# The first expert pair's tokens by a matrix product, three weight loads with other waits, and the combine between a pair's gates

## What is computed

```python
def hier_moe(h, rg_w, rg_b, re_w, re_b, w_gate, w_up, w_down):   # h = rmsnorm(x, ln_ffn)
    lg = tf @ rg_w + rg_b;  grp = argmax(lg)                      # one group of 4
    top_v, top_i = lax.top_k(le, 2)                               # two of its 8 experts
    combine = sum(one_hot(eid, 32) * (g1 * g2)[..., None])        # weight of each expert for each token
    for e in range(N_EXPERTS):                                    # 32 experts, D_MODEL 1024, D_EXPERT 512
        hid = silu(t @ w_gate[e]) * (t @ w_up[e])
        acc = acc + combine[:, e:e + 1] * (hid @ w_down[e])
    return acc
```

## Time and profile before

| | us |
|---|---|
| median of 3 runs (lowest, highest) | 820.41 (819.87, 823.77) |
| the profiled execution, its time | 821.48 |
| the profiled execution, its span | 819.8 |
| PE busy | 772.7 (94%) |
| DVE busy | 270.4 (33%) |
| ACT busy | 158.6 (19%) |
| POOL busy | 139.1 (17%) |
| queue q1 (SP's), share of the 16 DMA engines | 74.1% |

### The profile page before, as it was taken

The page is one execution under the profiler, slowest core; times in us unless marked ns, Lnnn a source line. Parts: engine busy times, 40 slices in busy tenths (PEclk is TensorE's granted clock), DMA queues, the critical chain, the costliest instruction groups (busy, mean ns, idle before and its releaser), DMA issues.

```text
span 819.8 us, 8712 instructions
## 1 busy us (share of the span) xinstructions
PE 772.7 (94%) x3488; PEld 372.7 (45%) x3488; DVE 270.4 (33%) x614; ACT 158.6 (19%) x313; POOL 139.1 (17%) x167
## 2 busy tenths in 40 slices
PE   4999999989999999889999999999998999899996
PEld 3777677758743334544333333333333333333332
DVE  2059999995355632521111101110110111011001
ACT  3211121234541101300211111111111111101114
POOL 2069899702002000010000000000000000000000
PEclk9999999999999999989999999999999999999999
DMA  9894200041508189989999999999999999999981
GB/s 275 301 350 166 103 20 0 2 110 41 167 26 265 57 276 348 419 320 427 426 426 426 427 429 424 427 429 425 426 426 428 426 426 427 427 428 426 429 335 65
DMA packets 51256, 249.58 MB, mean 304 GB/s; under 512 B 6966, under 2 KB 24406, under 8 KB 38655
## 3 DMA queue, kind: packets, MB, share of 16 engines
q1 hardware_dynamic: 45540, 243.54, 74.1%
q10 hardware_dynamic: 3147, 2.67, 1.1%
q0 software_dynamic: 2528, 2.79, 1.1%
HBM read 246.87 MB, written 8.61 MB: 312 GB/s over the span
## 4 chain that ended last, share of the span: by engine, by line
PE 71%; DVE 4%; issue 3%; ACT 2%; DMA 0%; DVEq 0%; ACTq 0%; POOLq 0%
PE bank L1177 27%; PE bank L1200 14%; PE bank L1051 9%; PE bank L1218 8%; PE bank L1160 2%; PE bank L1189 1%; PE bank L1024 1%; PE bank L1015 1%; DVE bank L1571 1%; PE bank L788 1%; PE bank L1178 1%; PE bank L1040 1%; PE bank L885 1%; DVE bank L1600 1%; DVE region_a L1570 1%
## 5 line engine op out<-in xcount | busy, mean ns | idle before, releaser
L788 PE MATMUL bank<-region_a,ring 128*128 128x320 f32 x576 | 158.7, 437 | 0.5 <-DVE region_a L1570 0.5
L1178 PE MATMUL bank<-ring,zz 128*64 128x512 f32 x304 | 135.3, 601 | 0.0
L788 PEld LDWEIGHTS bank<-region_a,ring 128*128 128x128 f32 x576 | 109.8, 192 | 46.5 <-issue 2.2
L1177 PE MATMUL bank<-ring,zz 128*64 128x512 f32 x272 | 122.9, 608 | 8.6 <-issue 8.0
L1570 DVE TENSOR_TENSOR region_a<-region_a,bank 64x512 f32<-64x512 f32 (+1 forms) x33 | 22.5, 680 | 328.6 <-ACT region_a L1497 328.4
L1571 DVE SCALAR_TENSOR_TENSOR bank<-region_a,par,bank 128x256 f32<-128x256 f32 x232 | 91.2, 483 | 0.0
L744 POOL DMA_INDIRECT region_a<-hn_scratch,region_a x16 | 15.9, 995 | 379.1 <-PE bank L1160 362.6
L1218 PE MATMUL bank<-zz,masks 128*128 128x512 f32 (+1 forms) x192 | 75.3, 609 | 2.1 <-ACT zz L1503 2.1
L1177 PEld LDWEIGHTS bank<-ring,zz 128*64 128x64 f32 x272 | 37.1, 140 | 83.7 <-issue 82.9
L1051 PE MATMUL bank<-ring,x_v_y 128*128 128x512 f32 (+1 forms) x192 | 74.1, 606 | 0.8 <-DVE x_v_y L1570 0.8
L1503 ACT ACTIVATE zz<-bank 64x512 f32<-64x512 f32 x64 | 37.8, 591 | 169.5 <-PE bank L1200 169.1
(11 more groups left out here) (310 smaller groups left out, 806.2 us busy)
## 6 DMA issues: line engine op xcount, KB each, us to landing
ring<-in_expert_w_up SPq DMA_DIRECT2D x19, 2048.0 KB, 33.7
ring<-in_expert_w_down SPq DMA_DIRECT2D x18, 2048.0 KB, 38.0
ring<-in_expert_w_gate SPq DMA_DIRECT2D x16, 2048.0 KB, 35.6
ring<-in_w_in SPq DMA_DIRECT2D x9, 2048.0 KB, 20.0
x_v_y<-in_expert_w_down SPq DMA_DIRECT2D x7, 2048.0 KB, 28.0
x_v_y<-in_expert_w_gate SPq DMA_DIRECT2D x5, 2048.0 KB, 42.5
ring<-in_w_out SPq DMA_DIRECT2D x4, 2048.0 KB, 9.1
xcx<-in_expert_w_gate SPq DMA_DIRECT2D x4, 2048.0 KB, 35.8
```

What stands on the lines that cost most here:

```text
L788: ins = pe.matmul(pt[0:m, 0:T], w[:, k, :], ht[:, k, :], start=k == 0, stop=k == KD - 1)
L1177: pe.matmul(to[0:CAP, :], x[:, k, :], wg[:, FE * k:FE * k + FE], **st)
L1178: ins = pe.matmul(to[CAP:P, :], x[:, k, :], wu[:, FE * k:FE * k + FE], **st)
```

## The change

It has three parts.

1. **The first two experts' tokens come from a product.** DVE makes a 0/1 selection `first` (token by slot, 64 slots of expert 0 and 64 of expert 1), scaled by each token's 1/rms, and PE multiplies the residual `xt` by it: 12 products of 128 x 128 for each half, in place of the gather for pair 0 and its eight transposes. `first` can be made from `rank`, without waiting for the list of slots. The gathers begin with pair 1.
2. **Loads 8, 9 and 10** wait for the logits, for `hn_out` and for `kept`; load 8 waited for `hn_out` too before, and load 9 for the first gather. The copies of the residual into the accumulators are spread: a half of `residual(1)` goes ahead of the rank counts, `residual(2)` behind them, and the other half of `residual(1)` to the very end of the routing.
3. **The combine** of the pair two back stands between the gates of the even and the odd expert, no longer between the two halves of the next tokens' transposes.

```diff
-    banks, prev, last, held, own = [], [], {}, {}, {}
+    banks, prev, last, held, own = [], [], {}, {}, {("rank",): 2, ("slots",): 2}
...
             sp_.wait_ge(filled, J[("lg2",)] + 1)
+            load_expert(n_slot - 3)
             sp_.wait_ge(S("hn_out"), 48)
-            load_expert(n_slot - 3)
-            sp_.wait_ge(S("gath"), 16)
             load_expert(n_slot - 2)
...
-            for i in range(NE // 2):
-                wait(pool, S("xg_T"), 2 * i)
+            for i in range(1, NE // 2):
+                if i > 1:
+                    pool.wait_ge(S("xg_T"), 2 * i)
                 pool.indirect_dma_start(gat, None, hn_dram[:, :],
...
             residual(0)
+            residual(1, [0])
             pe.wait_ge(S("chosen"), 1)
...
             counts(ones, 2, 3, start=False, stop=True).then_inc(filled, 1)
+            residual(2)
...
+            def first_tokens(h):
+                to = job_bank("tokens", (0, h))
+                for k in range(4):
+                    for r, (t0, n) in enumerate(TILES):
+                        if h == 0 and k == 0:
+                            pe.wait_ge(S("first"), r + 1)
+                        ins = pe.matmul(to[:, P * k:P * k + P], xt[0:n, r, 4 * h + k:D:KD], first[0:n, r, :],
+                                        start=r == 0, stop=r == 2)
+                ins.then_inc(S("xg_T"), 1)
+                return ins
...
+            first_tokens(0)
             pe.wait_ge(S("osel"), 1)
-            slot_values(take(pe, "slots")).then_inc(filled, 1)
-            residual(1)
-            residual(2).then_inc(S("kept"), 1)
+            slot_values(take(pe, "slots"), osel).then_inc(filled, 1)
+            first_tokens(1)
+            residual(1, [1]).then_inc(S("kept"), 1)
             after_read(pe, "slots")
...
-            pe.wait_ge(S("gath"), 16)
-            for h in range(2):
-                tokens_T(0, h)
-
             for i in range(NE // 2):
                 for e in (2 * i, 2 * i + 1):
+                    if i >= 2 and e % 2:
+                        combine(i - 2)
                     gate, up = expert_landed(pe, 0, e), expert_landed(pe, 1, e)
...
                 if more:
-                    pe.wait_ge(S("gath"), 16 * (i + 2))
-                    tokens_T(i + 1, 0)
-                if i >= 2:
-                    combine(i - 2)
-                if more:
-                    tokens_T(i + 1, 1)
+                    pe.wait_ge(S("gath"), 16 * (i + 1))
+                    for h in range(2):
+                        tokens_T(i + 1, h)
...
+            link(dve.tensor_scalar(first_off, aa[:, :, 0:2], -BIG, BIG, ALU.mult, ALU.add))
...
             pt = got(dve, "rank")
-            link(tt_(tee, ee, bc(r3(pt[:, 0:3 * NE]).unsqueeze(1), [P, 2, 3, NE]), ALU.mult))
+            link(tt_(first_at, r3(pt[:, 0:3 * NE])[:, :, 0:2], first_off, ALU.add))
+            for r, (t0, n) in enumerate(TILES):
+                for j in range(2):
+                    ins = dve.tensor_scalar(first[0:n, r, CAP * j:CAP * j + CAP], slotno[0:n, :],
+                                            first_at[0:n, r, j:j + 1], rst[0:n, 3 + r:4 + r],
+                                            ALU.is_equal, ALU.mult)
+                ins.then_inc(S("first"), 1)
+            tt_(tee, ee, bc(r3(pt[:, 0:3 * NE]).unsqueeze(1), [P, 2, 3, NE]), ALU.mult).then_inc(S("tee"), 1)
...
-            for h in range(2):
-                tokens(0, h)
+            tokens(0, 0)
+            pair_indices(got(dve, "slots")).then_inc(S("idx"), 1)
+            slot_indices(got(dve, "slots"))
+            pair_values(got(dve, "slots")).then_inc(free["dve"], 1)
+            tokens(0, 1)
```

30 lines of the change are left out of this document (16 added, 14 removed).

## The result

| | before | after |
|---|---|---|
| median of 5 runs each (lowest, highest), us | 823.60 (819.87, 823.77) | 829.70 (828.49, 832.87) |
| the profiled execution, its span, us | 819.8 | 826.8 |
| start of the first gate, us | 358.67 | 369.79 |
| load 10 issued, us | 357.37 | 369.89 |
| gate 30 to the first down product behind gate 31, us | 20.5 | 18.4 |

The changed kernel takes 1.0087 times the time of the one before (95% interval 1.0065 to 1.0109): it is slower, where I had forecast 6.1 us less. (The ratio is taken over all runs side by side; the two medians of the table alone give 1.0074, which lies in the interval too.) The span grew by 7.0 us.

The account below looks back on a forecast made before the run. The stream of expert matrices at 427 GB/s bounds the kernel until expert 31, then PE. Savings 3.2 + 0.8 + 2.1 = 6.1 us take the profiled 821.48 to 815.4, median 814.3 us, range 812.2 to 817.6.

Parts of the forecast that it names:

- The dent and its mechanism: Stream from 348 to 360 us: late issues of loads 8 and 9 lose 5.3 us; issuing them earlier closes it.
- The start of the first gate: End of routing: new product takes 2.9 us a half, so the first gate starts at 358.5 us, 358.67 before.
- The clock decides: PE before the first gate: gapless work raises the clock near 351 us; a half costs 2.9 or 5.1 us.
- The bound of 360.1: Latest first gate considered for the clock, in us, if it rises only at 354.3; slow-front rival, chance 0.14.
- The rival on the weight loads: New product: weight loads do not overlap, 48 rows cost 5.1 us more, gate at 363.6, total 819.4 us; chance 0.04.
- Is the queue ever empty behind load 10: Stream behind the first gate: it stays busy, load 13 going 2.7 us early, more than the 1.7 needed.
- the formula: Stream gain d = 361.7 minus the first gate's start, plus 0.8 and 2.1 us at the kernel's end.
- Part 3: Last pair: combine fills the pause between gates, gate 30 to down product 18.4 us, 2.1 less; gate 30 gains 0.8.
- The pair without a wait: PE-bound pairs take 27.7 us, under the stream's 29.5; PE first waits for a matrix beyond 720 us.
- slower: the pair grows: Rival: moving the combine exposes 1.65 us in each of 13 pairs, total 826.2 us; chance 0.05.
- the clock dip at the end: Rival: PE's wait ahead of gate 30 lowers the clock, costing 2.1 us, total 816.4 us; chance 0.13.
- the late `hn`: Rival: load 8 holds up the write of `hn`, leaving a 1.8 us gap, total 816.1 us; chance 0.05.

Follow-up runs that it names:

- e8: Changed kernel with the new product's loops turned, its stationary operand contiguous and experts 0 and 1 loaded in matching channel order; 0.9925 of the kernel before, 816.53 us.
- e1: The kernel before with only the combine moved between a pair's gates; 0.9966 of the kernel before, 819.97 us beside 822.16.
- e2: Changed kernel with 128 neighbouring columns as the new product's stationary operand, loops unchanged; 0.9996 of the kernel before.
- e6: Changed kernel with the new product's loops turned and its stationary operand contiguous, outputs not the reference's; 0.9896 of the kernel before.
- e5: Changed kernel with the new product's loops turned (token tiles outside, channels inside), stride kept; 1.0005 of the kernel before.
- e9: e8 with the changed kernel's loops (channels outside) and the third tile zero-padded from 64 to 128 rows; 0.9919 of the kernel before.

## Why the prediction was wrong, point by point

- **The dent and its mechanism: right.** Loads 8 and 9 went when forecast (load 9 0.5 us sooner) and cost nothing; the stream then hung on load 10 alone, as the sum had it.
- **The start of the first gate: wrong, and this is the step that failed.** "The scan's products of exactly this form took 3.82 us for 32 rows at full clock, 0.119 us each, so 2.9 us for each half". The form was the same only in the shapes that the row prints: 128 x 128 by 128 columns. The stride of the stationary operand and the tiles of 64 rows between those of 128 are not in it, but both were plain in the diff (`4 * h + k:D:KD`, and `xt[0:n, r, ...]` over TILES). The term measured 7.94 + 8.15 = 16.1 us, not 5.8: 6.2 us by the stride and 4.4 by the changes of the row count (which hold 1.4 of the fallen clock). The change could have been read beforehand: in the trace of before, at 354.9 us, the first row of 64 among the residual's copies starts 0.522 us behind the last of 128, where rows of 512 columns are else 0.43 apart.
- **"The clock decides": the right question with too narrow an answer.** I bounded the product by the two clock levels, 2.9 and 5.1 us a half, as if only the clock could change its price, and took it that work without a gap would raise the clock near 351 us. It was high from 345.6 us on, and fell at 352.4, during gapless work. The strided rows cost 0.240 us at either level, so the clock was not what set their price. The bound of 360.1 for the first gate was passed by 9.7 us. Two readings were a little off as well, and change nothing: 0.68 in the microsecond from 354 us puts the rise of before at 354.6, not 354.3, and 349.3 + 0.9 + 7.6 is 357.8, not 357.5.
- **The rival on the weight loads: right direction, wrong mechanism, half the size.** It gave 5.1 us for 48 rows at full clock and 363.6 for the gate. The product does take 10.3 us over the forecast, but by the stride of its loads and at the changes of the row count; loads on the same rows as the running product do overlap. I gave it 0.04 because the scan's rows spoke against it, and they did not bear on this operand.
- **"Is the queue ever empty behind load 10": right for e8** (halves of loads 11 and 12 released 3.7 us behind the gate's start, forecast 3.4, and 427 GB/s from 372 to 780 us), **wrong for the changed kernel**, where gate 0 began at half clock and load 13 went 15.5 us behind its start, not 13.8. The step assumed gate 0 at full clock without a row for it; behind that gate lie the 1.8 us that the formula leaves.
- **Part 3: right.** 18.42 us from gate 30 to the down products (forecast 18.4), and e1 gives 0.9966 for it alone: 2.8 us of 822, beside 0.8 + 2.1 = 2.9.
- **The pair without a wait: right.** Loads released by the same product of pairs 3 and 4 go 27.8 us apart in the changed kernel (418.72 and 446.52; forecast 27.7), and PE first waits for a matrix at 746 us, as forecast "beyond 720".
- **The rival "slower: the pair grows", the clock dip at the end, the late `hn`: none came in the changed kernel.** (The dip is real: in e2 the clock fell from 745.7 to 749.1 us behind a wait of 2.2 us ahead of gate 28. It did not reach the end: gate 30 came 406.4 us behind the first gate, in the changed kernel 406.3.) The forecast gave "slower" 0.06 and named only a pair that grows for it. A rival "the new product takes as long as its slowest like" would have been the one to price; by the formula, any first gate later than 364.6 us makes the kernel slower (361.7 + 0.8 + 2.1).

## What to carry to other kernels

Price a new product by its operands' strides and by the sequence of its row counts, not only by the shape that the profile prints; where no row of the trace has the same stride, take the nearest price as the lower end and a multiple of it for the upper (here it was 2.8 times: 16.1 for 5.8). Where one semaphore ahead of a full queue stands behind a stage (here `kept`), that stage's time is paid one for one at the end as long as the queue runs empty there (e6, e5), so the last thing to put ahead of it is a product with an unknown price. Short independent work put into the pause between two matrices of a stream-bound pair is nearly free, and its gain could be read from the timeline beforehand.

## What was not expected of the hardware

- At full clock a weight load of 128 x 128 float32 took 337 ns with a stride of 32 bytes (e5) and 192 ns without (e6), and rows came 0.240 us apart instead of 0.111; transposes with the same stride had loads of 193 ns. At half clock strided rows stayed at 0.240 us (e5, the changed kernel) and contiguous ones took 0.213 (e2, e9).
- Between products over 128 and over 64 rows 0.2 us were lost at each change at full clock (e6, e8) and 0.3 at half clock (e2, e5); padding the 64 with zeros avoided it (2.95 us for 24 rows, though it works on more rows).
- The granted clock fell to 0.50 while PE worked without a gap, at 352.4 us in the changed kernel, and stayed there for 20.5 us; with rows at 0.111 us it stayed at 1.00 in e6 and e8, but fell for 3.4 us in e9. The cause was not tested.
- Weight loads of 2 MiB in pieces of 2 KB were slower than with 16 KB: load 1 took 10.6 us from issue to landing in e8 and 9.2 before, and load 7, behind four such loads, landed 1.4 us later though it was issued at the same time (336.34 and 336.35 us).
